# Memory columns and key weights in three parts, norm weights first on the queue, token scale spread later

## The chip, the core and the metric

The kernel runs on one core of a Trainium2 chip. The metric is the device time of one execution in microseconds (us). Three runs of the kernel before gave 1145.51, 1147.50 and 1147.76 us, a median of 1147.5.

The core's engines work in parallel, each through its own list of instructions: TensorE (PE, matmuls), VectorE (DVE), ScalarE (ACT), GpSimd (POOL) and SyncE (SP, which here issues nearly all transfers from memory). They meet through semaphores.

## What is computed

An encoder trunk of two layers over 256 tokens of width 1024, in fp32. Cut to what matters here:

```python
mem_n = rms_norm(mem, mem_norm)
for i in range(DEPTH):                       # 2 layers
    h = rms_norm(x, norm_mix[i])
    mkv = mem_n @ w_mem_kv[i]                # keys and values of the memory
    if i % 2 == 0:
        u = h @ na_w_in[j]                   # neighbourhood attention, layer 0
        ...
    else:
        mix, mq = gla_mixer(...)             # gated linear attention, layer 1
    att = memory_attention(mq, mkv)
    x = x + jnp.concatenate([mix, att], axis=-1) @ w_out[i]
    x = x + hierarchical_moe(rms_norm(x, norm_ffn[i]), ...)   # 32 experts, 2 per token
return rms_norm(x, final_norm)
```

The norm of a token is a factor for the token (the scale) times a weight for each feature. The kernel applies the two at different times: the weight to the transposed activations as soon as they are there, the scale of the memory tokens only to the keys and values that come out.

## The kernel before

The weights, about 440 MB, are read once. They pass through a ring in on-chip memory of eleven slots of 2 MB. SP issues the transfers in the order of use and waits before each for its slot; PE counts up `ring_used` as it finishes with weights.

The feature dimension of 1024 is cut into eight chunks of 128 (`KC`, index k). The memory tokens come as columns, `memT` (chunk by chunk, 256 tokens each), and are multiplied by key weights `mem_kw0` in `mem_k(0)` (L791 to L809). Columns and key weights arrive in two halves: chunks 0 to 3, then 4 to 7, in four transfers of 512 KB (L574 to L577). DVE multiplies chunks 0 to 3 by the norm weights, two at a time (L2096 to L2098), ACT chunks 4 to 7, one at a time (L1674 to L1677). PE waits for the DVE parts with `n_hT`, for all of ACT's with `n_hTa`, and for the key weights with `landed_kv0`. The norm weights of all norms, `gcol`, 28 KB, are the first transfer that ACT issues (L1460); a part of the constants (`cst`, with the identity and the matrix of ones) is its second.

PE's order at the start: four matmul calls on zeros (L1192 to L1195), `mem_k(0)`, `mem_v(0)` (L818 to L833: memory values, in two tiles of 128 tokens, eight chunks each), the memory queries (L1199 to L1205), the memory scale in every row (L1206, `scale_rows(1, 3)`), then the token values of attention (L838). Between the two tiles of `mem_v(0)` stands `scale_rows(0, TOKENB)` (L811 to L816). It waits for two diagonal matrices that DVE makes of the token scales (L1867), which rest on ACT's sums of squares over the token rows `xres` (L1496), and multiplies them by ones, so that every row holds the scale of all tokens. DVE needs this to scale and weight the eight chunks of token columns `hT0` (L2103 to L2108); the memory queries wait for chunks 0 to 3 and then for chunks 4 to 7 of them.

Behind the memory part SP issues, in this order: memory values' weights, token rows, token columns, query weights, memory rows, constants, value weights (L688 to L695), the weights of queries and keys (L698) and more. `piece_in` holds three semaphores for pieces of the last expert weights of each layer; PE waits for them at L1144 and L1146, long after the start.

fp32 matmul calls show as two instructions each in the trace.

Of the kernel before, what the change touches and what calls it, by code (L numbers as in the profile page):

```python
# [14 lines left out]
T = 256  # L15
# [42 lines left out]
TOKENB = 4  # L58
# [122 lines left out]
def build(nc, x, mem, final_norm, gla_out_norm, moe_w1, moe_w3, moe_w2, consts, mem_columns, x_columns, mem_keys, mem_values, mem_queries0,  # L181
          values0, queries_keys0, values1, values1_second, mem_queries1, queries_keys1, gates1, out0, out1, gains,
          logit_weights, logit_biases, gate_biases, gate_ups, biases0, first_up, last_up, last_down, out):
    with ExitStack() as ctx:
        def sb(name, shape, dt=F32):
            return ctx.enter_context(nc.sbuf_tensor(name, shape, dt))

        def sem(name):
            return ctx.enter_context(nc.semaphore(name))


        ring = sb("ring", [P, SLOTS * SLOT])
        cst = sb("cst", [P, C_END])
        gcol = sb("gcol", [P, 7, KC])
# [140 lines left out]
        s_x, s_mem, s_cst, s_rpb, s_small = sem("x_in"), sem("mem_in"), sem("const_in"), sem("rpb_in"), sem("small_in")  # L335
        s_gain = sem("gains_in")
# [12 lines left out]
        ring_in = [sem(f"ring_in{i}") for i in range(SLOTS + 1)]  # L349
# [58 lines left out]
        rt_p = sem("positions")  # L408
        rt_n = sem("rounds")
        again = [sem(f"positions_kept_and_last_group_selected_again{i}") for i in range(2)]  # L410
        piece_in = [sem(f"{name}_in") for name in ("third_slice_half0", "third_quarter", "third_slice_last_quarter")]

        class Quads:

# [31 lines left out]
        def quarter_columns(slot):  # L446
            return slot_view(slot).rearrange("p (q j e n) -> p q j e n", q=2, j=2, e=E4)
# [123 lines left out]
        @block.sync  # L571
        def _(sp):
            memT_rows = memT.rearrange("p k t -> p (k t)")
            for half in range(2):  # L574
                c, w = slice(half * 4 * T, (half + 1) * 4 * T), slice(half * 4 * 256, (half + 1) * 4 * 256)
                sp.dma_start(memT_rows[:, c], mem_columns[:, c]).then_inc(ring_in[(10, 9)[half]], 16)
                sp.dma_start(ring[:, w], mem_keys[0][:, w]).then_inc(ring_in[(8, 0)[half]], 16)  # L577

            def free(l, n):

# [189 lines left out]
        def _(pe):  # L770
            def arrived(a):
                pe.wait_ge(*a)
# [18 lines left out]
            def mem_k(l):  # L791

                w = mem_kw0 if l == 0 else kw1
                if l == 0:
                    arrived(landed_kv0[0])
                else:
                    arrived(landed_k1)
                    pe.wait_ge(s_memT, 1)
                for k0 in (0, 4):
                    if l == 0 and k0 == 4:  # L800
                        arrived(landed_kv0[1])
                        pe.wait_ge(n_hTa, TT)
                    for m in range(MPAIR):
                        for k in range(k0, k0 + 4):
                            if (l, m) == (0, 0) and k in (0, 2):
                                pe.wait_ge(n_hT, k // 2 + 1)
                            t = pe.matmul(ps[:, KB[l], m * T:(m + 1) * T], w[:, k, m * P:(m + 1) * P], memT[:, k, :],
                                          start=(m, k) == (0, 0), stop=(m, k) == (MPAIR - 1, KC - 1))
                t.then_inc(kv_mm, 1)  # L809

            def scale_rows(nth, bank):  # L811

                for a in range(TT):
                    pe.wait_ge(s_diag0, TT * nth + a + 1)
                    t = pe.matmul(ps[:, bank, a * P:(a + 1) * P], ones, diag0[:, a, :], start=True, stop=True)
                t.then_inc(s_rbc0, 1)  # L816

            def mem_v(l):  # L818

                w = mem_vw[l]  # L820
                if l == 0:
                    pe.wait_ge(s_memv, 16)
                else:
                    slot, there = main[0].fill(0, KV_AT * FILLS)
                    pe.wait_ge(ring_in[slot], there)
                for a in range(TT):
                    if l == 0 and a == 1:
                        pe.wait_ge(s_cst, 16)
                        scale_rows(0, TOKENB)
                    for k in range(KC):  # L830
                        t = pe.matmul(ps[:, VB[l], a * 256:a * 256 + 256], memT[:, k, a * P:(a + 1) * P], w[:, k, :],  # L831
                                      start=k == 0, stop=k == KC - 1)
                t.then_inc(ring_used, 1)  # L833
# [281 lines left out]
            def last_pieces(rn, l, c, slot, there):  # L1115

                w = quarter_columns(slot)
# [23 lines left out]
                pe.wait_ge(rn.sig.selwT_ready, c + 1)  # L1141
                pe.wait_ge(rn.sig.yb_ready, c * 2 + l + 1)
                scatter(rn, 0, 512, PIECES[0][3])
                pe.wait_ge(piece_in[1], 16 * (l + 1))  # L1144
                piece(1, 1).then_inc(rn.sig.down_half, 1)
                pe.wait_ge(piece_in[2], 16 * (l + 1))  # L1146
                piece(2, 0)
                if l == 0:
                    pe.wait_ge(rn.sig.added, c * 4 + 1)
# [307 lines left out]

        @block.scalar
        def _(act_e):
            act_e.dma_start(gcol[:], gains).then_inc(s_gain, 16)  # L1460
            act_e.dma_start(cst[:, 0:256], consts[:, 0:256]).then_inc(s_cst, 16)
            def table(func):

# [368 lines left out]
        def _(dve):  # L1832
# [261 lines left out]
            dve.wait_ge(s_gain, 16)  # L2094
            dve.wait_ge(ring_in[10], 16)
            for k in (0, 2):  # L2096
                V.tensor_tensor(memT[:, k:k + 2, :], memT[:, k:k + 2, :],
                                gcol[:, GAIN[0], k:k + 2].unsqueeze(2).to_broadcast([P, 2, T]), ALU.mult).then_inc(n_hT, 1)  # L2098
            dve.wait_ge(s_cst, 16)
# [95 lines left out]
            for i in range(2):  # L2195
                r, c = slice(i * CH, (i + 1) * CH), slice(i * CH, (i + 1) * CH)
# [72 lines left out]
```

## Time and profile before

| | |
|---|---|
| median of three runs | 1147.5 us (1145.51 to 1147.76) |
| span of the profiled execution | 1146.5 us |
| PE busy | 855.9 us (75%) |
| DVE busy, ACT busy | 208.9 us (18%), 179.1 us (16%) |
| moved by DMA | 444.48 MB, mean 388 GB/s |
| mean granted clock of TensorE | 0.881 |

The profile is of one execution. A busy share is a mean over stages with different limits, so it does not say what an edit in one stage is worth; for that the stage's own rows are read. A timeline row gives the start, the length, the engine, the line, what is written and read, and how many instructions were merged; in brackets stands how long the engine was idle ahead of it and what ended that. Matmuls overlap their successors, so that the distance between two starts tells more than the length of a row. A granted clock of 1.00 is 2.4 GHz, 0.50 is 1.2 GHz.

### The profile page before, as it was taken

The page shows a single profiled execution, that of the slowest core. Times are in us where ns is not written, and L with a number is a line of the kernel's source. Part 1 is how long each engine was busy: PE and PEld are TensorE (multiplying, and loading weights), DVE is VectorE, ACT ScalarE, POOL GpSimd, SP SyncE. Part 2 cuts the span into 40 slices and gives each one's busy share as a digit, 9 for nine tenths or more (in the row PEclk, how much of TensorE's full clock was granted, in tenths as well). Part 3 has the DMA queues.
Part 4 walks back from the last instruction along what each step waited for, and adds up shares of the span by engine and source line. Part 5 has one row for each costly group of instructions (what it writes and reads, how often), then busy time and mean ns, then how long its engine had stood idle before and what let it go on. Part 6 is the DMA issues. An engine that isn't in the chain of part 4 may idle for free.

```text
span 1146.5 us, 11577 instructions
## 1 busy us (share of the span) xinstructions
PE 855.9 (75%) x5102; PEld 401.9 (35%) x5102; DVE 208.9 (18%) x402; ACT 179.1 (16%) x384; POOL 19.2 (2%) x20
## 2 busy tenths in 40 slices
PE   9999997674948376757799999976565665664677
PEld 7687553221413121212258666322121221221222
DVE  2223231010101010101016634211010101010011
ACT  3333111010101000000036432100010100000002
POOL 0500000000000000000000000000000000000000
PEclk9999998896988778888999999988787888888887
DMA  9973799999999999999995658999999999999996
GB/s 375 420 297 112 281 380 412 429 429 428 426 427 428 428 425 428 430 429 427 421 424 216 258 222 334 421 428 428 428 428 427 429 427 426 428 428 427 428 426 245
DMA packets 36857, 444.48 MB, mean 388 GB/s; under 512 B 4545, under 2 KB 5057, under 8 KB 8002
## 3 DMA queue, kind: packets, MB, share of 16 engines
q1 hardware_dynamic: 36224, 443.16, 92.4%
q8 instruction: 43, 0.70, 0.2%
q10 hardware_dynamic: 578, 0.52, 0.1%
q14 instruction: 12, 0.10, 0.0%
HBM read 442.62 MB, written 1.05 MB: 387 GB/s over the span
## 4 chain that ended last, share of the span: by engine, by line
PE 53%; DMA 41%; ACT 2%; issue 2%; DVE 1%; SPq 0%; DVEq 0%
DMA ring<-in_moe_w 35%; PE ps L1026 12%; PE ps L1030 9%; PE ps L838 5%; PE ps L1235 4%; PE ps L917 3%; PE ps L998 3%; PE ps L1012 3%; DMA ring<-in_last_up 3%; DMA ring<-in_last_down 2%; PE ps L1325 2%; PE ps L924 2%; PE ps L1291 1%; DMA xres<-in_x 1%; PE ps L831 1%
## 5 line engine op out<-in xcount | busy, mean ns | idle before, releaser
L1026 PE MATMUL ps<-ring,work 128*32 128x512 f32 x2032 | 255.3, 658 | 138.3 <-DMA ring<-in_moe_w 117.1
L1030 PE MATMUL ps<-ring,work 128*32 128x512 f32 (+1 forms) x1024 | 141.8, 714 | 107.8 <-DMA ring<-in_moe_w 104.4
L1026 PEld LDWEIGHTS ps<-ring,work 128*32 128x32 f32 x2032 | 75.9, 119 | 303.3 <-issue 284.4
L1030 PEld LDWEIGHTS ps<-ring,work 128*32 128x32 f32 x1024 | 38.6, 131 | 200.0 <-issue 192.7
L2056 DVE TENSOR_TENSOR xres<-xres,ps 128x512 f32<-128x512 f32 (+1 forms) x64 | 42.9, 671 | 295.5 <-PE ps L998 292.9
L1012 PE MATMUL ps<-xs,work 128*128 128x512 f32 x112 | 54.5, 632 | 11.9 <-issue 9.5
L998 PE MATMUL ps<-work 128*128 128x512 f32 x120 | 55.7, 606 | 0.4 <-ACT work L1612 0.4
L838 PE MATMUL ps<-ring 128*128 128x384 f32 x160 | 53.3, 489 | 0.0
L2047 DVE TENSOR_TENSOR work<-work,ps 128x512 f32<-128x512 f32 x16 | 11.0, 688 | 231.9 <-PE ps L1026 231.9
L1625 ACT COPY work<-ps 128x512 f32<-128x512 f32 x28 | 16.4, 585 | 219.4 <-PE ps L1030 219.4
L1603 ACT COPY work<-ps 128x256 f32<-128x256 f32 x16 | 5.9, 372 | 247.6 <-PE ps L1063 247.6
L1235 PE MATMUL ps<-ring 128*128 128x256 f32 x192 | 43.0, 382 | 0.0
L917 PE MATMUL ps<-ring 128*128 128x512 f32 x88 | 39.1, 595 | 0.0
L1235 PEld LDWEIGHTS ps<-ring 128*128 128x128 f32 x192 | 36.0, 190 | 5.8 <-issue 0.9
L2018 DVE TENSOR_TENSOR work<-ps,gcol 128x512 f32<-128x512 f32 (+1 forms) x34 | 20.9, 655 | 92.3 <-PE ps L1017 90.0
L838 PEld LDWEIGHTS ps<-ring 128*128 128x128 f32 x160 | 29.8, 190 | 20.8 <-issue 1.4
L1012 PEld LDWEIGHTS ps<-xs,work 128*128 128x128 f32 x112 | 22.4, 203 | 42.0 <-issue 38.4
L998 PEld LDWEIGHTS ps<-work 128*128 128x128 f32 x120 | 21.5, 189 | 34.0 <-issue 34.0
L2044 DVE TENSOR_TENSOR work<-work,ps 128x512 f32<-128x512 f32 x16 | 11.0, 687 | 118.7 <-ACT work L1601 118.7
L1601 ACT ACTIVATE work<-ps 128x512 f32<-128x512 f32 x16 | 9.6, 597 | 138.0 <-PE ps L1026 138.0
L1599 ACT COPY work<-ps 128x512 f32<-128x512 f32 x28 | 16.4, 585 | 89.7 <-PE ps L1012 89.7
L917 PEld LDWEIGHTS ps<-ring 128*128 128x128 f32 x88 | 16.2, 190 | 18.0 <-issue 18.0
(273 smaller groups left out, 688.3 us busy)
## 6 DMA issues: line engine op xcount, KB each, us to landing
ring<-in_moe_w SPq DMA_DIRECT2D x161, 2048.0 KB, 30.8
ring<-in_last_up SPq DMA_DIRECT2D x8, 2048.0 KB, 34.3
ring<-in_moe_w SPq DMA_DIRECT2D x14, 1024.0 KB, 6.7
ring<-in_first_up SPq DMA_DIRECT2D x5, 2048.0 KB, 11.6
ring<-in_out SPq DMA_DIRECT2D x4, 2048.0 KB, 27.5
ring<-in_last_down SPq DMA_DIRECT2D x4, 2048.0 KB, 36.1
ring<-in_queries_keys SPq DMA_DIRECT2D x7, 1024.0 KB, 25.8
ring<-in_first_up SPq DMA_DIRECT2D x4, 1024.0 KB, 7.6
```

The source lines that it names most:

```text
L838: t = pe.matmul(ps[:, bank, 0:w.shape[-1]], hTs[l][:, k, a * P:(a + 1) * P], w[:, k, :], start=k == 0, stop=k == KC - 1)
L917: t = pe.matmul(ps[:, WOB[l][a] + half, :], mixTs[l][:, c, a * P:(a + 1) * P], out_rows(l, c, half), start=c == first, stop=c == last)
L924: t = pe.matmul(ps[:, WOB[l][1] + half, :], mixTs[l][:, c, P:2 * P], out_rows(l, c, half), start=False, stop=c == 5)
L998: pe.matmul(ps[:, banks[a], 0:n], selwT[:, a, :], yb[:, c0:c0 + n], start=True, stop=True).then_inc(rn.sig.scattered, 1)
L1012: t = pe.matmul(ps[:, half, :], sel[:, a].rearrange("p e s -> p (e s)"), xs[:, a, half * 512:half * 512 + 512], start=a == 0, stop=a == TT ...
L1026: return pe.matmul(ps[32 * e:32 * e + 32, 4 + m, :], xsel[:, k, 32 * e:32 * e + 32], w, start=k == 0, stop=k == KC - 1, tile_position=(0, ...
L1030: return pe.matmul(ps[32 * e:32 * e + 32, bank, 0:w.shape[-1]], actT[:, j, 32 * e:32 * e + 32], w, start=j == 0, stop=j == 3, tile_positio ...
L1235: t = pe.matmul(ps[:, p % 2, t_ * T:(t_ + 1) * T], qkw[p][t_][:, k, :], hT0[:, k, :], start=k == 0, stop=k == KC - 1)
L1325: t = pe.matmul(ps[:, 4 + j, t_ * T:(t_ + 1) * T], qkw1[t_][j][:, k, :], hT1[:, k, :], start=k == 0, stop=k == KC - 1)
L1599: nc.scalar.copy(xrow[:, half * 512:half * 512 + 512], ps[:, half, :]).then_inc(rn.sig.picked_sb, 1)
L2018: V.tensor_tensor(xsel[:, k0:k0 + n, :], ps[:, bank, 0:n * P].rearrange("p (k t) -> p k t", t=P), gcol[:, 2 + 2 * l, k0:k0 + n].unsqueeze( ...
L2056: V.tensor_tensor(cols, cols, ps[:, banks[a], 0:n], ALU.add).then_inc(rn.sig.added, 1)
```

## The change

The norm weights move from ACT's first issue to SP's first issue, ahead of the memory columns. The memory columns and key weights come in three parts, chunks 0-1, 2-3 and 4-7, six transfers instead of four. The second parts report on two of the `piece_in` semaphores, which are renamed and whose later waits count 16 higher. DVE waits for the second columns before its second operation, PE for the second keys before chunk 2. `mem_k` runs in three parts for both layers. `scale_rows(0, TOKENB)` moves from ahead of tile 1 of the memory values to behind the first four chunks of that tile.

```diff
@@ sync @@
-            for half in range(2):
-                c, w = slice(half * 4 * T, (half + 1) * 4 * T), slice(half * 4 * 256, (half + 1) * 4 * 256)
-                sp.dma_start(memT_rows[:, c], mem_columns[:, c]).then_inc(ring_in[(10, 9)[half]], 16)
-                sp.dma_start(ring[:, w], mem_keys[0][:, w]).then_inc(ring_in[(8, 0)[half]], 16)
+            sp.dma_start(gcol[:], gains).then_inc(s_gain, 16)
+            for (k0, k1), mem_there, keys_there in (((0, 2), ring_in[10], ring_in[8]), ((2, 4), s_mem2, s_keys2),
+                                                    ((4, 8), ring_in[9], ring_in[0])):
+                c, w = slice(k0 * T, k1 * T), slice(k0 * 256, k1 * 256)
+                sp.dma_start(memT_rows[:, c], mem_columns[:, c]).then_inc(mem_there, 16)
+                sp.dma_start(ring[:, w], mem_keys[0][:, w]).then_inc(keys_there, 16)
@@ tensor, mem_k @@
-                for k0 in (0, 4):
+                for k0, k1 in ((0, 2), (2, 4), (4, 8)):
+                    if l == 0 and k0 == 2:
+                        pe.wait_ge(s_keys2, 16)
                     if l == 0 and k0 == 4:
                         arrived(landed_kv0[1])
                         pe.wait_ge(n_hTa, TT)
                     for m in range(MPAIR):
-                        for k in range(k0, k0 + 4):
+                        for k in range(k0, k1):
@@ tensor, mem_v @@
                 for a in range(TT):
-                    if l == 0 and a == 1:
-                        pe.wait_ge(s_cst, 16)
-                        scale_rows(0, TOKENB)
                     for k in range(KC):
+                        if l == 0 and (a, k) == (1, 4):
+                            pe.wait_ge(s_cst, 16)
+                            scale_rows(0, TOKENB)
@@ tensor, last pieces @@
-                pe.wait_ge(piece_in[1], 16 * (l + 1))
+                pe.wait_ge(piece_in[1], 16 * (l + 2))
...
-                pe.wait_ge(piece_in[2], 16 * (l + 1))
+                pe.wait_ge(piece_in[2], 16 * (l + 2))
@@ scalar @@
-            act_e.dma_start(gcol[:], gains).then_inc(s_gain, 16)
@@ vector @@
             for k in (0, 2):
+                if k == 2:
+                    dve.wait_ge(s_mem2, 16)
                 V.tensor_tensor(memT[:, k:k + 2, :], memT[:, k:k + 2, :],
```

## Rows read from the trace of the kernel before

**Rows 1.** The page, part 4: chain that ended last, shares by engine.

```profile
PE 53%; DMA 41%; ACT 2%; issue 2%; DVE 1%; SPq 0%; DVEq 0%
```

**Rows 2.** Stretches: span, length, each engine's busy us, clock, DMA share, GB/s.

```profile
core 0: us, PE busy (x) PEld busy (x) DVE busy (x) ACT busy (x) POOL busy (x), PEclk, DMA share, GB/s
0.00:55.00 55.00, 52.75 (x215) 37.12 (x216) 13.84 (x30) 18.32 (x43) 17.20 (x17) 1.00 0.98 397
...
113.00:154.00 41.00, 40.44 (x179) 23.15 (x174) 14.55 (x45) 11.62 (x24) 0.00 (x0) 1.00 0.79 309
...
215.00:570.00 355.00, 226.77 (x1397) 81.49 (x1397) 37.52 (x62) 25.43 (x46) 0.00 (x0) 0.83 1.01 427
...
585.00:695.00 110.00, 109.85 (x551) 74.85 (x550) 49.06 (x61) 45.22 (x91) 1.97 (x3) 1.00 0.69 274
```

**Rows 3.** Waits of SP's queue, 50 to 250 us: us, times, longest.

```profile
SPq L666 <- PE ps L860: 13.4, 1, 13.4
```

**Rows 4.** Timeline of PE, first 8 us: start, us, what [idle before].

```profile
5.08 1.33 PE L1195 MATMUL ps<-work 128*128 128x256 f32 x4
6.85 1.35 PE L807 MATMUL ps<-work,ring 128*128 128x256 f32 x5 [0.44 <-DMA ring<-in_mem_keys]
```

**Rows 5.** Timeline of PE, 13 to 30 us.

```profile
13.86 3.62 PE L831 MATMUL ps<-ring,work 128*128 128x256 f32 x16
17.32 0.38 PE L815 MATMUL ps<-work,cst 128*128 128x128 f32 x2
17.96 0.49 PE L815 MATMUL ps<-work,cst 128*128 128x128 f32 x2 [0.26 <-DVE work L1867]
18.29 3.62 PE L831 MATMUL ps<-ring,work 128*128 128x256 f32 x16
21.74 7.07 PE L1203 MATMUL ps<-ring 128*128 128x256 f32 x32
28.65 0.61 PE L815 MATMUL ps<-work,cst 128*128 128x128 f32 x4
29.09 1.13 PE L838 MATMUL ps<-ring 128*128 128x384 f32 x3
```

**Rows 6.** Timeline, 0 to 60 us: scaling by DVE and ACT, the last diagonal.

```profile
5.40 1.29 DVE L2097 TENSOR_TENSOR work<-work,gcol 128x512 f32<-128x512 f32 x2 [3.94 <-DMA gcol<-in_gains]
...
8.30 1.70 ACT L1675 ACTIVATE work<-work,gcol 128x256 f32<-128x256 f32 x4 [5.13 <-DMA work<-in_mem_columns]
...
17.62 0.29 DVE L1867 TENSOR_SCALAR work<-cst,st 128x128 f32<-128x128 f32 x1
...
18.56 3.22 DVE L2105 SCALAR_TENSOR_TENSOR ring<-ring,gcol,ps 128x256 f32<-128x256 f32 x8 [0.65 <-PE ps L815]
```

**Rows 7.** Timeline of SP's issues: first columns, second columns, second keys.

```profile
0.75 0.38 SPq L576 DMA_DIRECT2D work<-in_mem_columns  x1
...
1.66 0.42 SPq L576 DMA_DIRECT2D work<-in_mem_columns  x1
2.13 0.58 SPq L577 DMA_DIRECT2D ring<-in_mem_keys  x1
```

**Rows 8.** Line 576, memory columns: from issue to landing.

```profile
DMA to landing us min/median/max: 4.4/5.5/6.5
```

**Rows 9.** Line 577, key weights: from issue to landing.

```profile
DMA to landing us min/median/max: 5.6/6.5/7.3
```

**Rows 10.** Stretch of half a microsecond, columns as in rows 2.

```profile
2.00:2.50 0.50, 0.50 (x1) 0.00 (x1) 0.00 (x0) 0.50 (x1) 0.00 (x0) 1.00 0.75 198
```

**Rows 11.** Line 695, value weights, issued from 6.15 us: from issue to landing.

```profile
DMA to landing us min/median/max: 21.6/22.8/24.0
```

**Rows 12.** Line 735, first store of the output: from issue to landing.

```profile
DMA to landing us min/median/max: 2.0/2.0/2.0
```

**Rows 13.** Timeline of PE: up projection at 161 us and in the tail.

```profile
161.68 7.08 PE L1026 MATMUL ps<-ring,work 128*32 128x512 f32 x64
...
1115.87 3.64 PE L1026 MATMUL ps<-ring,work 128*32 128x512 f32 x16 [1.81 <-DMA ring<-in_last_up]
```

More of the change, by code:

```diff
@@ L410, in build @@
         again = [sem(f"positions_kept_and_last_group_selected_again{i}") for i in range(2)]
-        piece_in = [sem(f"{name}_in") for name in ("third_slice_half0", "third_quarter", "third_slice_last_quarter")]
+        piece_in = [sem(f"{name}_in") for name in ("third_slice_half0", "memory_columns_2_3_then_third_quarter",
+                                                   "memory_keys_2_3_then_third_slice_last_quarter")]
+        s_mem2, s_keys2 = piece_in[1], piece_in[2]
         class Quads:
```

## Prediction

> **What bounds the kernel now.** I read the chain of work that ended last first: PE 53%, DMA 41% [rows 1]. The split by stage says which holds where [rows 2]: in 0 to 55 us PE is busy for 52.75 us at a granted clock of 1.00 (the 2.4 GHz level), and so it is in 113 to 154 and 585 to 695; in 215 to 570 the DMA share is 1.01 at 427 GB/s and PE is busy for 227 of 355 us: there the expert weights set the pace. The change touches only the first 30 us, a stage set by PE. Does a microsecond won there reach the end, with a stage behind it that is bound by DMA? In 113 to 154 the DMA share is only 0.79, since SP waits for ring slots that PE frees; the longest such wait for the next stream of weights is 13.4 us, for the last transposes of attention [rows 3]. So the long stream starts when PE lets it, and what PE gains early moves the stream, and then all behind it, by the same amount.
>
> Next the first 30 us of PE, in order of time [rows 4, 5]. Warm-up matmuls run to 6.41. The first memory matmul starts at 6.85, after 0.44 us of idle that ended with the landing of the key weights. Then 32 instructions (16 matmul calls, two each) run without a gap, at (13.86 - 6.85) / 32 = 0.22 us each. The memory values take 16 instructions (tile 0), 13.86 to 17.32; then come the four instructions that spread the token scale. The second pair of them waits for DVE; tile 1 starts at 18.29, which is 0.97 us after 17.32. The same four instructions without a wait take 29.09 - 28.65 = 0.44 us. So this wait costs PE 0.53 us. The memory queries (L1203) start at 21.74. The whole visible idle that the change can take is therefore 0.44 + 0.53 = 0.97 us.
>
> **Part 1: smaller transfers and norm weights first.** Before, DVE scaled memory chunks 0 to 3 at 5.40 to 6.69, released by the norm weights, not by the columns (issued at 0.75, landed 4.4 us later, 5.15) [rows 6 to 8]. With only chunks 0 and 1 in front (256 KB and 256 KB instead of 512 and 512) the first keys no longer wait for the second half of their own transfer. The two landings in the queue before were 512 KB apart and 1.2 to 1.6 us apart: columns 5.15, keys 6.8, columns 1.66 + 6.5 = 8.16, keys 2.13 + 7.3 = 9.43 [rows 4, 7 to 9]. Half of that spacing is 0.6 to 0.8 us for 256 KB, so the first keys should land near 5.2 to 5.6, under the warm-up's end at 6.41, the DVE operation of 0.65 us before it too. PE then starts at 6.41, or, since matmul records overlap their successors, as early as 6.25 (last warm-up matmul at 6.03 plus 0.22). Chunks 2 and 3 are needed 8 instructions later, at 8.0 to 8.2; they land where the first MB landed before, near 6.8, and are scaled before that. Nothing stalls.
>
> What is late next is the third part. ACT scales chunks 4 to 7 in four operations, 8.30 to 10.00, and starts when the columns land (8.16) [rows 6, 8]. PE reached them at 6.85 + 16 x 0.22 = 10.4 before, so ACT was covered by 0.4 us. Now PE would be there at 9.8 to 10.0 and waits for ACT until 10.05. Hence the gain at this point is 10.43 - 10.05 = 0.38 us, not 0.44 to 0.6, less every delay d of the third columns. The third keys (9.43 + d) are in time for d below 0.6.
>
> How large is d? The bytes ahead of the third columns are the same; what is new is three more issues on SP, 0.44 us each [rows 7]: the third columns are issued about 1.3 us later (norm weights, then five transfers). Lower bound 0: they already took 6.5 us from issue to landing, nearly all of it behind other bytes. Upper bound 1.3: the issue time decides in full. In between: the queue is short of work only in its first microseconds, when it moved 198 GB/s against 397 on average over 0 to 55 [rows 2, 10]. The one issue put ahead of the first columns costs at about half rate 0.44 x 0.5 = 0.2 us. The third columns' row is nearer to the lower bound, since the queue is never empty again, so d = 0.2. All later transfers (token rows, token columns, values) shift by the same d.
>
> A rule of the Trainium skill speaks against this part. The trace shows a smallest time from issue to landing of 2.0 us, for an output store on an idle queue [rows 12], yet landings in a filled queue 1.2 to 1.6 us apart. "DMA: Bandwidth & Descriptors", section "Rules for kernel authors", asks for at least 1 MiB per DMA, and the section on the anatomy of one DMA gives a fixed 2.0 us for each. If each paid that alone, an estimate from that page would be 3 x 2.0 = 6 us of delay; the landing rows do not bear it out, as four transfers would then be over 2 us apart.
>
> **Part 2: token scale spread later.** It moves behind the first four chunks of tile 1, 8 instructions or 1.73 us later on PE. The values of tile 0 start at 13.86 - 0.38 + d = 13.48 + d, tile 1 at 16.94 + d, the scale at 18.67 + d. The diagonals are ready at 17.91 + d [rows 6], so the wait of 0.53 us is gone, with 0.76 us to spare. But DVE's scaling of the token columns (L2105, eight operations in 3.22 us) starts later: before it came 0.11 us after the end of the second pair (17.96 + 0.49 = 18.45); all four in a row last 0.61. That is 18.67 + 0.61 + 0.11 = 19.39 + d, against 18.56. Four of eight are done at 19.39 + 1.61 = 21.00 + d, and 0.06 for the signal (my estimate from DVE's end at 17.91 and PE's start at 17.96) makes 21.06 + d. PE itself is done with tile 1 at 18.67 + 0.44 + 1.73 = 20.84 + d. So a small new wait of 0.22 us stands ahead of L1203, on DVE. The second four are done at 22.67 + d, and PE wants them at 21.06 + 1.73 = 22.79 + d: just in time. L1203 starts at 21.06 + d instead of 21.74: the sum is -0.68 + d, with d = 0.2 **-0.48 us**.
>
> Behind it: L838 needs the second half of the values, which landed at 6.15 + 21.6 = 27.8 [rows 11]; PE asks now at 28.6 (29.09 before). With d = 0.2 it lands at 28.0: covered by 0.6 us. The two new waits of PE (chunks 2 and 3) and the split loop, also run once for layer 1 with the same 32 instructions, cost 0 to 0.1 us; I take 0. ACT's second issue starts 0.44 us earlier and its constants are wanted only for the diagonals, of which the last is made at 17.62: nothing. The other counts of the reused semaphores cost nothing: the same waits at the same places.
>
> The profiled execution has a span of 1146.5 us; the median of the runs is 1147.5, so about 1.0 lies around the span. 1146.5 - 0.48 = 1146.0, plus 1.0 gives 1147.0 us.
>
> **Rivals.**
> (a) The issues decide (d from 0.4 to 1.3). At d = 0.68 the gain is gone: the third columns land at 8.84 or later and PE stands before them. At d = 1.3 the kernel is slower by 0.62: 1148.1. For it: six issues of 0.44 us one after another. Against it: 6.5 us from issue to landing. Chance 0.16.
> (b) Slower by more than can be overlooked: every transfer pays its own start. With 2.0 us from the store's row for each of the three additional ones, d = 6.0, and L1203 comes 5.3 us later: 1152.8. It decides from d = 0.68 and passes 0.2% of the time from d = 3.0. This is also the time by the skill's rule. The spacing of landings speaks against it: 0.03.
> (c) The gain does not reach the end: somewhere between 120 and 215 us the stream is kept by its own bytes. Then 1147.5. The 13.4 us wait of SP speaks against it: 0.09.
> (d) TensorE's clock in the tail. The last L1026 group runs 16 instructions in 3.64 us, at a granted clock of 0.50 (1.2 GHz), right after PE's waits for the last weights; the same form took 7.08 us for 64 at 1.00, so 1.77 for 16 [rows 13]. A shift of all events by 0.5 us may move the fall or rise of the clock. If it does not fall, this group gains 1.87 us and the next ones some 1.3: 1143.7. Chance 0.06. If it rises only after 1133 instead of 1125, up to 7 us of full-rate work runs slower, half of it taken: 1150.5. Chance 0.05.
>
> **How the numbers follow.** The forecast, -0.68 to -0.28, has the remaining 0.61. A measurement of this kernel can tell about 0.2% (2.3 us) from no change; its own runs span 2.25 us. Forecast, (a) and (c) lie within that; (d) has 0.06 below and 0.05 above, (b) 0.03 above; the runs' scatter adds 0.05 to faster and leaves 0.01 for slower. So faster 0.11, same 0.80, slower 0.09. The range takes the scatter about the forecast and (a): 1144.4 to 1149.0.
>
> **What would show it.** PE's first memory matmul at 6.25 to 6.45, no idle to DMA; a short idle ahead of its 17th instruction, ended by ACT L1675 or its columns; the four scale instructions without idle between them, from about 18.9; DVE's L2105 at 19.6; L1203 at 21.26 with about 0.2 us of idle; the wait of SP for the last transposes ending about 0.5 us earlier than 124.3. A third landing of columns after 9.0 would show (a); landings 2 us apart (b). A time beyond the range would have to come with another pattern of clock, or with a DMA rate other than 427 GB/s in the long stretches; then my claim that only the shift matters is wrong.

## Result: slower by 0.2%, from transfers that land late in the first microseconds

In 15 runs each, the changed kernel took 1148.98 us in the median (1145.8 to 1152.07) and the kernel before 1147.32 us (1144.49 to 1148.96). The ratio is 1.0019, with a 95% interval of 1.0010 to 1.0027: slower by 1.1 to 3.1 us. I had forecast 1147.0 and a small gain. The time lies just inside my range, but the movement goes the other way and is clear of the noise.

PE's timeline in the changed kernel shows where it begins (start, length, instructions, idle before; it answers to [rows 4, 5]):

```profile
5.90 1.89 PE L813 MATMUL ps<-work,ring 128*128 128x256 f32 x8
8.64 2.00 PE L813 MATMUL ps<-work,ring 128*128 128x256 f32 x8 [0.85 <-DMA ring<-in_mem_keys]
12.07 3.69 PE L813 MATMUL ps<-work,ring 128*128 128x256 f32 x16 [1.44 <-ACT work L1680]
15.60 5.34 PE L837 MATMUL ps<-ring,work 128*128 128x256 f32 x24
20.78 0.61 PE L821 MATMUL ps<-work,cst 128*128 128x128 f32 x4
21.22 1.89 PE L837 MATMUL ps<-ring,work 128*128 128x256 f32 x8
23.30 7.15 PE L1209 MATMUL ps<-ring 128*128 128x256 f32 x32 [0.18 <-DVE ring L2112]
```

PE starts the memory keys at 5.90 instead of 6.85, a gain of 0.95 us. Eight instructions later it waits for the second keys, and eight later again for ACT. The third part starts at 12.07, 1.7 us after the time (about 10.4) at which the kernel before had reached the same chunks. The token scale runs without a wait, as intended, and L1209, the memory queries, starts at 23.30 instead of 21.74. The loss is in the landings of the transfers. ACT and the token rows, with SP's issues (answering to [rows 6, 7]):

```profile
0.75 0.38 SPq L576 DMA_DIRECT2D gcol<-in_gains  x1
1.19 0.42 SPq L580 DMA_DIRECT2D work<-in_mem_columns  x1
1.66 0.42 SPq L581 DMA_DIRECT2D ring<-in_mem_keys  x1
...
3.08 0.43 SPq L580 DMA_DIRECT2D work<-in_mem_columns  x1
...
10.22 1.70 ACT L1680 ACTIVATE work<-work,gcol 128x256 f32<-128x256 f32 x4 [7.53 <-DMA work<-in_mem_columns]
16.43 1.06 ACT L1501 ACTIVATE xs<-xres 128x1024 f32<-128x1024 f32 x1 [4.50 <-DMA xres<-in_x]
```

ACT's scaling of the last columns starts at 10.22 (8.30 before), the first work on the token rows, when they land, at 16.43 (14.54 before). So the last memory columns and the token rows behind them land 1.9 us later, and so do the memory rows (ACT's work on them starts at 23.98 instead of 22.09). The stretches of two microseconds show when the queue fell behind (columns as in [rows 2]). Before:

```profile
4.00:6.00 2.00, 2.00 (x5) 1.14 (x4) 0.60 (x1) 0.00 (x0) 0.00 (x0) 1.00 1.00 381
6.00:8.00 2.00, 1.56 (x7) 1.06 (x7) 0.69 (x2) 0.00 (x0) 0.00 (x0) 1.00 1.02 384
8.00:10.00 2.00, 2.00 (x11) 1.74 (x11) 0.00 (x0) 1.70 (x4) 0.00 (x0) 1.00 1.05 438
```

And after:

```profile
4.00:6.00 2.00, 2.00 (x7) 1.20 (x6) 0.69 (x1) 0.00 (x0) 0.00 (x0) 1.00 0.89 271
6.00:8.00 2.00, 1.78 (x9) 1.23 (x7) 0.69 (x1) 0.00 (x0) 0.00 (x0) 1.00 0.79 215
8.00:10.00 2.00, 1.36 (x6) 1.23 (x7) 0.00 (x0) 0.00 (x0) 0.00 (x0) 1.00 1.04 409
```

Between 2 and 4 us the changed kernel was ahead (287 GB/s against 205). Between 4 and 8 us its queue moved 215 to 271 GB/s instead of 381 to 384, and the DMA engines were busy only 0.79 to 0.89 of the time, though SP had issued more than 2 MB by then. Idle engines are only part of it: 215 GB/s at a share of 0.79 would be 272 at a full share, against 376 before (384 / 1.02), so the engines also moved fewer bytes while they were busy. From 8 us on the rates are nearly the same again.

The bytes account for about half of the 1.9 us. Over the first 20 us the queue moved 331 GB/s on average, against 352 before, which is 0.42 MB less, or 1.0 us at the 410 to 430 GB/s of the stretches behind; over the first 30 us (361 against 375) it is still 0.42 MB. The other half is order. When the token rows landed, 5.13 MB had been moved in the changed kernel (312 GB/s over 16.43 us) and 4.77 MB before (328 over 14.54), although the bytes needed until then are the same: more of the later transfers was already done. No run shows why.

From there the delay goes with PE. SP's wait for the last transposes is the same 13.4 us as in [rows 3], only later (it ends at 125.92 instead of 124.29), the first expert matmul starts at 155.74 instead of 154.12, the long stretches run at the same rate (427 GB/s), and the tail's L1032 group starts 1.94 us later than in [rows 13]. The two profiled executions nevertheless have the same span, 1146.5 us. The tail says why. After:

```profile
1117.81 3.55 PE L1032 MATMUL ps<-ring,work 128*32 128x512 f32 x16 [2.97 <-DMA ring<-in_last_up]
...
1123.67 1.93 PE L1036 MATMUL ps<-ring,work 128*32 128x512 f32 x24 [0.68 <-ACT work L1610]
```

Before, the second of these groups was

```profile
1122.20 3.42 PE L1030 MATMUL ps<-ring,work 128*32 128x512 f32 x24 [0.68 <-ACT work L1605]
```

The same 24 instructions took 1.93 us in one execution and 3.42 in the other: the granted clock was back at 1.00 (2.4 GHz) from 1122 on after, and only from about 1125 on before. The two small groups ahead of it gained as well. What decides this is open: the second trace of the changed kernel has 1.93 us too, and of the 14 other kernels below eight have the short group and six a long one of 3.0 to 3.6 us, with the same matmuls in the tail of all. The medians do not share the gain.

### The profile page after: what moved, and what is told of

Same layout as the page of the kernel before. It is cut to its first block, busy times and chain, and to the rows that moved or that the text cites. A ratio compares the mean times of both kernels' runs of the same rounds, so it can differ in the third digit from the quotient of the medians.

```text
span 1146.5 us, 11580 instructions
## 1 busy us (share of the span) xinstructions
PE 861.0 (75%) x5102; PEld 403.1 (35%) x5102; DVE 209.1 (18%) x402; ACT 179.1 (16%) x384; POOL 19.2 (2%) x20
## 4 chain that ended last, share of the span: by engine, by line
PE 49%; DMA 47%; ACT 1%; DVE 1%; issue 1%; SPq 0%; DVEq 0%; ACTq 0%
DMA ring<-in_moe_w 41%; PE ps L1032 13%; PE ps L1036 8%; PE ps L844 5%; PE ps L1241 4%; PE ps L923 3%; DMA ring<-in_last_up 3%; DMA ring<-in_last_down 2%; PE ps L1331 2%; PE ps L1004 2%; PE ps L930 2%; PE ps L1018 1%; PE ps L1297 1%; PE ps L813 1%; PE ps L949 1%
## 5 line engine op out<-in xcount | busy, mean ns | idle before, releaser
L1032 PE MATMUL ps<-ring,work 128*32 128x512 f32 x2032 | 262.1, 673 | 131.6 <-DMA ring<-in_moe_w 111.1
L1036 PE MATMUL ps<-ring,work 128*32 128x512 f32 (+1 forms) x1024 | 138.3, 699 | 107.7 <-DMA ring<-in_moe_w 104.6
L1032 PEld LDWEIGHTS ps<-ring,work 128*32 128x32 f32 x2032 | 77.3, 122 | 302.1 <-issue 283.9
L1018 PE MATMUL ps<-xs,work 128*128 128x512 f32 x112 | 57.6, 663 | 11.5 <-issue 9.2
```

Of the source, the lines that this page charges most:

```text
L1018: t = pe.matmul(ps[:, half, :], sel[:, a].rearrange("p e s -> p (e s)"), xs[:, a, half * 512:half * 512 + 512], start=a == 0, stop=a == TT ...
L1032: return pe.matmul(ps[32 * e:32 * e + 32, 4 + m, :], xsel[:, k, 32 * e:32 * e + 32], w, start=k == 0, stop=k == KC - 1, tile_position=(0, ...
L1036: return pe.matmul(ps[32 * e:32 * e + 32, bank, 0:w.shape[-1]], actT[:, j, 32 * e:32 * e + 32], w, start=j == 0, stop=j == 3, tile_positio ...
```

## Experiments

Two markers of a trace do not depend on the tail: the time at which the token rows land (ACT's first work on them) and the start of the first expert matmul. In three kernels with the same transfers as before (the kernel before, `e3_scale_later`, `e6_pe_delay`) the token rows landed at 14.54, 14.67 and 14.83, so 0.3 us is the scatter of the first marker. A difference from the one trace of the kernel before can be too large by as much. The bytes moved in the first 20 us scatter less: these three kernels have a mean of 351 to 352 GB/s, so they are the third marker, "queue".

The texts on record name theories by letters. P: packets of 2 KB are slow. N: each additional issue of SP delays all behind it. G: norm weights ahead of the columns hold the queue up. W: each transfer over all engines costs the queue 0.5 to 0.8 us at the start. T: the moment at which the first megabyte stands in the queue decides. S: transfers of 256 KB are slower at the start. C: the two queues disturb each other. The diffs show only the lines that matter, with "..." where lines are left out.

All numbers of the experiments (us; "queue" in GB/s):

| kernel | token rows | last columns scaled from | memory queries | first expert matmul | queue | ratio (95%) |
|---|---|---|---|---|---|---|
| before | 14.54 | 8.30 | 21.74 | 154.12 | 352 | |
| after | 16.43 | 10.22 | 23.30 | 155.74 | 331 | 1.0019 (1.0010 to 1.0027) |
| f3_after_again | 16.24 | 10.03 | 23.10 | 155.74 | 327 | 1.0016 (1.0002 to 1.0030) |
| e1_gains_first | 15.38 | 9.15 | 22.57 | 154.94 | 344 | 1.0014 (1.0001 to 1.0027) |
| e2_three_parts | 15.70 | 9.46 | 22.90 | 155.55 | 333 | 1.0011 (1.0000 to 1.0022) |
| e3_scale_later | 14.67 | 8.46 | 21.54 | 153.99 | 351 | 1.0001 (0.9988 to 1.0014) |
| e4_rows_split | 17.08 | 10.86 | 25.58 | 158.08 | 307 | 1.0028 (1.0014 to 1.0042) |
| e5_keys_on_act | 16.36 | 11.36 | 25.20 | 157.77 | 343 | 1.0024 (1.0013 to 1.0036) |
| e6_pe_delay | 14.83 | 8.60 | 24.94 | 157.76 | 352 | 1.0026 (1.0016 to 1.0037) |
| e7_small_packets | 14.14 | 7.92 | 21.34 | 153.72 | 357 | 1.0002 (0.9991 to 1.0014) |
| e8_tiny_issues | 14.53 | 8.32 | 21.73 | 154.63 | 352 | 1.0009 (0.9996 to 1.0022) |
| f1_five_tiny | 15.08 | 8.85 | 22.28 | 154.65 | 349 | 1.0004 (0.9992 to 1.0015) |
| f2_small_wide | 15.04 | 8.80 | 22.23 | 154.98 | 346 | 1.0004 (0.9994 to 1.0014) |
| e9_best | 14.29 | 8.06 | 21.66 | 154.12 | 350 | 1.0005 (0.9997 to 1.0014) |
| g1_slow_first_mb | 15.24 | 9.02 | 22.44 | 155.07 | 339 | 1.0007 (0.9995 to 1.0018) |
| g2_after_cst_late | 16.97 | 10.72 | 23.80 | 156.24 | 317 | 1.0012 (0.9998 to 1.0026) |
| g3_second_half_split | 15.37 | 8.38 | 22.57 | 155.25 | 346 | 1.0008 (0.9996 to 1.0020) |

In `g3_second_half_split` 8.38 is for chunks 4 and 5; chunks 6 and 7 are scaled from 9.65.

### The parts of the change one by one

`e1_gains_first`: only the norm weights' place.

```diff
+            sp.dma_start(gcol[:], gains).then_inc(s_gain, 16)      # SP, first
-            act_e.dma_start(gcol[:], gains).then_inc(s_gain, 16)   # ACT, first
```

> The kernel before with one part of the change alone: the norm weights are SP's first issue instead of ACT's; still two halves of columns and keys, scale spread early. The disputed number is the start of ACT's scaling of the last columns, which follows their landing: 8.30 us before, 10.22 after, with L1203 (memory queries) at 21.74 and 23.30. Theory P (the packets of 2 KB of the small transfers are slow): no such packets here, ACT starts at 8.3 to 8.5 and memory queries at 21.2 to 21.7. Theory N (each additional issue of SP delays all that stands behind it): one issue more, 0.44 us, so ACT at 8.6 to 8.8. Theory G (norm weights ahead of the columns hold the queue up): ACT at 9.5 to 10.2. Total within 0.1% of before by P and N, up to 2 us slower by G.

Measured: token rows at 15.38, last columns scaled from 9.15. This is between N and G: 0.84 us for one issue of 0.44 us, or 0.55 against the latest of the three traces with unchanged transfers (14.83).

`e2_three_parts`: only the six transfers instead of four, with the waits that go with them.

```diff
-            for half in range(2):
+            for (k0, k1), mem_there, keys_there in (((0, 2), ...), ((2, 4), ...), ((4, 8), ...)):
```

> The kernel before with the three parts of columns and keys alone: six transfers, norm weights still issued by ACT, scale spread early. P and N: nearly the whole loss is here, ACT's scaling starts at 9.6 to 10.2, memory queries at about 23 to 23.7 (no gain from a later scale, but the wait for the diagonals is hidden as PE is late itself); the total is 1.2 to 2.5 us slower. G: ACT at 8.3 to 8.7, memory queries at 21.7 to 22.

Measured: token rows 15.70 (1.16 us later), scaling from 9.46, memory queries 22.90. The two parts add up within the scatter: 0.84 + 1.16 = 2.0 against 1.89 for the whole change. So "nearly the whole loss is here" was wrong; the norm weights carry about two fifths of it. The stretch from 6 to 8 us shows that idle engines are not needed for the loss:

```profile
6.00:8.00 2.00, 2.00 (x10) 1.73 (x9) 0.69 (x1) 0.00 (x0) 0.00 (x0) 1.00 0.94 224
```

The engines were busy for 0.94 of it and moved 224 GB/s, where the kernel before moved 384 at 1.02.

`e3_scale_later`: only the later spread of the token scale.

```diff
-                    if l == 0 and a == 1:
...
+                        if l == 0 and (a, k) == (1, 4):
```

> The kernel before with the token scale spread behind four chunks of tile 1, and nothing else. All theories of the loss lie in the transfers, so this alone should gain: scale instructions without a wait at 19.05, memory queries at 19.05 + 0.61 + 0.11 + 1.61 + 0.06 = 21.44 instead of 21.74, and at 154 us the experts' first matmuls 0.3 us earlier. In the total 0.3 us cannot be told from nothing (ratio 0.999 to 1.001).

```profile
19.02 0.61 PE L815 MATMUL ps<-work,cst 128*128 128x128 f32 x4
19.46 1.89 PE L831 MATMUL ps<-ring,work 128*128 128x256 f32 x8
21.54 7.14 PE L1203 MATMUL ps<-ring 128*128 128x256 f32 x32 [0.18 <-DVE ring L2105]
```

PE's timeline of this kernel: no wait at the scale, a new one of 0.18 us on DVE ahead of L1203, and L1203 0.20 us earlier than before, experts 0.13. The mechanism of part 2 holds, its worth is 0.1 to 0.2 us, and the total shows nothing.

### Does PE's start reach the end?

`e6_pe_delay`: PE delayed alone, the transfers as before.

```diff
-            for _ in range(2):
+            for _ in range(12):
                 pe.matmul(ps[:, 7, 0:256], zeros[:, 0:P], zeros[:, 0:256], start=True, stop=True)
```

> The kernel before with ten more warm-up matmul calls of 256 columns on zeros (20 instructions at 0.22 us, 4.4 us), which only delay PE: the transfers stay as they are. PE's first memory matmul moves from 6.85 to about 10.65, memory queries from 21.74 to about 25.0, the first expert matmuls from 154.1 to 157.4. If PE's start sets the start of the long weight stream, as the prediction says, the total is 3.3 us slower (ratio 1.0028); the rival is that the stream goes by its own bytes, and then the total stays (ratio 0.999 to 1.001).

Memory queries at 24.94 (3.20 us later), experts 3.64 us later, total 1.0026 (1.8 to 4.2 us). PE's delay passes through. The rival "the gain does not reach the end", (c) of the prediction, falls.

### What makes the landings late?

`e7_small_packets`: packets of 2 KB, but no additional transfer.

```diff
+                        sp.dma_start(dst[:, 0:1024].rearrange("p (b n) -> p b n", b=2), blocks[:, 0:4:3]).then_inc(there, 16)
```

> The kernel before with four transfers of 512 KB in the same order, but the two first halves are read from memory in two pieces of 2 KB per row (blocks of two chunks stored in another order, results unchanged), so their packets are 2 KB, as in the change; no additional issue. Theory P: ACT's scaling of the last columns starts at 9.0 to 9.6 instead of 8.30, memory queries at 22.5 to 23. Theory N: 8.3 to 8.5 and 21.6 to 21.9.

Token rows at 14.14, scaling from 7.92, the earliest of all kernels. The packets of the first halves were of 2 KB here too and nothing was lost, so the theory of the small packets falls.

`e4_rows_split`: the same count and sizes of transfers as in the change, but packets of 4 KB, since the first halves are cut by partitions.

```diff
+            for half, rows, mem_there, keys_there in ((0, slice(0, 64), ...), (0, slice(64, 128), ...), (1, slice(0, 128), ...)):
```

> The kernel before with its first halves of columns and keys each cut by partitions (64 and 64) instead of by chunks: six transfers of the same sizes as in the change, issued in the same places, but each row keeps its 4 KB; both parts are awaited together, norm weights on ACT, scale early. It tells the packets' size from the number of transfers. P: the last columns land as before, ACT's scaling at 8.3 to 8.7, memory queries at 21.7 to 22.0. N: as with the three parts, ACT at 9.6 to 10.2 and memory queries at 23 or later.

Token rows at 17.08, later still than with the three parts. It speaks against P, but it does not count cleanly for N, because a transfer over 64 partitions is slow by itself:

```profile
4.00:6.00 2.00, 2.00 (x5) 1.08 (x4) 0.00 (x0) 0.00 (x0) 0.00 (x0) 1.00 1.07 204
6.00:8.00 2.00, 0.85 (x3) 0.27 (x1) 0.00 (x0) 0.00 (x0) 0.00 (x0) 1.00 1.04 221
```

Here the engines are fully busy (1.04 to 1.07) and move about half the bytes; in the changed kernel they are idle in part as well.

`e5_keys_on_act`: the changed kernel with the key weights issued by ACT.

```diff
-                sp.dma_start(ring[:, w], mem_keys[0][:, w]).then_inc(keys_there, 16)
+                act_e.dma_start(ring[:, k0 * 256:k1 * 256], mem_keys[0][:, k0 * 256:k1 * 256]).then_inc(keys_there, 16)
```

> The changed kernel with the three key transfers issued by ACT instead of SP (norm weights and columns stay on SP): the same six transfers with the same packets, but two engines issue at once, so the last columns are issued at about 2.1 us instead of 3.08, and all that SP issues behind them 1.4 us earlier. ACT's scaling of the last columns started at 10.22 in the changed kernel. Theory N (the issues of SP set the pace): it starts at 8.8 to 9.3, memory queries at 22 instead of 23.3. Theory P (packets of 2 KB, or the number of transfers in the queue whoever issues them): 9.8 to 10.3, memory queries at 23 or later.

All theories missed. The token rows land as in the changed kernel (16.36 against 16.43) although SP issued them 1.1 us earlier (3.50 against 4.58), and the columns come later. By then ACT had issued all keys (the third ones at about 1.7), so that they may have shared the engines with the columns; that is my reading and was not tried by itself:

```profile
9.62 0.69 DVE L2105 TENSOR_TENSOR work<-work,gcol 128x512 f32<-128x512 f32 x1 [3.39 <-DMA work<-in_mem_columns]
11.36 1.70 ACT L1681 ACTIVATE work<-work,gcol 128x256 f32<-128x256 f32 x4 [7.21 <-DMA work<-in_mem_columns]
```

The memory queries, at 25.20, carry more than this: PE waited 2.12 us for the second columns, and from 12 to 14 us the granted clock was 0.50.

`e8_tiny_issues` and `f1_five_tiny`: two or five transfers of 4 bytes between the halves.

```diff
+                if half == 0:
+                    for i in range(2):      # 5 in f1
+                        sp.dma_start(tiny[0:1, i:i + 1], consts[0:1, i:i + 1]).then_inc(s_out, 16)
```

> The kernel before with two transfers of 4 bytes each issued by SP between the first and the second half, which nobody waits for during the work: two more issues of about 0.44 us, no more bytes, packets of 4 KB. Theory N: ACT's scaling of the last columns starts 0.9 to 1.2 us later, at 9.2 to 9.5, memory queries at 22.6 to 23. Theory P: 8.3 to 8.5 and 21.7.

> The kernel before with five transfers of 4 bytes between the halves, on one partition each, so each uses one DMA engine: the last columns are issued at about 3.2 us, even later than in the changed kernel (3.08), and nothing is added to the other fifteen engines. Theory N (issue time decides, with a threshold that the two tiny ones did not pass): ACT's scaling of the last columns starts at 9.5 to 10.3 and the token rows land 1.5 us later. Theory W (each whole transfer, spread over all 16 engines, costs the queue 0.5 to 0.8 us in its first microseconds; single-engine ones cost nothing): ACT at 8.3 to 8.7, memory queries at 21.7 to 22.1.

With two, the last columns were issued at 2.30 and nothing landed later (14.53), which refutes N for two issues. With five:

```profile
1.67 1.64 SPq L581 DMA_DIRECT2D tiny<-in_consts  x5
3.35 0.36 SPq L577 DMA_DIRECT2D work<-in_mem_columns  x1
```

The last columns are issued at 3.35, later than in the changed kernel, and yet they are scaled from 8.85 and the token rows land at 15.08: 1.69 us of delay in the issue cost 0.54 (0.25 against the latest trace with unchanged transfers), and the mean over 20 us fell only from 352 to 349 GB/s. N and W both missed (9.5 or more, 8.7 or less). A late issue behind a full first megabyte is mostly hidden. This also refutes my rival (a) in its simple form.

`f2_small_wide`: two transfers of 18 KB over all partitions in the same place.

```diff
+                if half == 0:
+                    sp.dma_start(rbias[:, 0], logit_biases[:, 0]).then_inc(s_small, 16)
+                    sp.dma_start(rbias[:, 1], logit_biases[:, 1]).then_inc(s_small, 16)
```

> The kernel before with its logit biases, 36 KB, moved between the halves and cut in two, so that two small transfers over all 128 partitions and 16 engines stand there: 18 KB each, 36 KB more ahead of the last columns (0.1 us at 400 GB/s), last columns issued 0.9 us later. Theory W: ACT's scaling of the last columns starts at 9.3 to 10.0, like that of the three parts alone (9.46). If only bytes and the size of the data transfers count: 8.4 to 8.6. Theory N: 8.3 to 8.5 too, since two tiny issues did not delay it.

Token rows at 15.04 and scaling from 8.80, as with five tiny ones and later than the 8.4 to 8.6 for bytes alone. The two cost 0.50 us together, so a fixed price of 0.5 to 0.8 us for each whole transfer, as theory W had it (scaling from 9.3 or later), is not there.

`f3_after_again`: the changed kernel, a second trace.

> The changed kernel once more, for a second trace of its first microseconds. If the late landing belongs to the kernel, ACT's scaling of the last columns starts at 9.9 to 10.5 again and memory queries at 23.0 to 23.6, and the total is 1.5 to 3 us slower than before; if it was a chance of one execution, ACT starts at 8.3 to 9.5.

It repeats: 16.24, 10.03, 23.10, ratio 1.0016. The late landing belongs to the kernel.

`g1_slow_first_mb`: four transfers of 512 KB, but issued at the pace of the three parts.

```diff
+                for i in range(2) if half == 0 else ():      # between first columns and first keys
+                    sp.dma_start(tiny[0:1, i:i + 1], consts[0:1, i:i + 1]).then_inc(s_out, 16)
                 sp.dma_start(ring[:, w], mem_keys[0][:, w]).then_inc(ring_in[(8, 0)[half]], 16)
+                if half == 0:
+                    sp.dma_start(tiny[0:1, 2:3], consts[0:1, 2:3]).then_inc(s_out, 16)
```

> The kernel before with two transfers of 4 bytes (one engine each) between the first columns and the first keys, and one behind the keys: the four data transfers stay 512 KB, but the first megabyte is all issued only at 2.1 us and the last columns at about 2.6, the schedule that the three parts have. Token rows landed at 14.54 us before and 15.70 with the three parts. Theory T (the moment at which the first megabyte stands in the queue decides, about 1 us for each): token rows at 15.3 to 15.9, ACT's scaling of the last columns at 9.2 to 9.7. Theory S (transfers of 256 KB are themselves slower at the start than ones of 512 KB): 14.7 to 15.1 and 8.4 to 8.9, as with five tiny ones behind the first megabyte (15.08).

```profile
4.00:6.00 2.00, 2.00 (x5) 1.13 (x4) 0.86 (x2) 0.00 (x0) 0.00 (x0) 1.00 1.03 365
6.00:8.00 2.00, 1.66 (x9) 1.13 (x8) 0.43 (x1) 0.00 (x0) 0.00 (x0) 1.00 0.81 227
```

Token rows at 15.24. Its first keys were issued at 1.83 instead of 1.19, its last columns at 2.55, so earlier than in `f1_five_tiny` (3.35). The loss at the token rows, 0.70 us against 0.54 there, does not separate the two, since 0.16 us is less than the scatter. The bytes do: 339 GB/s over 20 us against 349, which is 0.6 us of work lost against 0.15, and there is the same hole between 6 and 8 us as in the changed kernel (227 GB/s at a share of 0.81), which `f1_five_tiny` does not have:

```profile
4.00:6.00 2.00, 2.00 (x5) 1.08 (x4) 0.37 (x1) 0.00 (x0) 0.00 (x0) 1.00 1.01 385
6.00:8.00 2.00, 1.80 (x7) 1.14 (x6) 0.92 (x2) 0.00 (x0) 0.00 (x0) 1.00 1.02 363
```

The value lies just under the span of T (15.3 to 15.9) and above that of S. If the two kernels may be compared so, the schedule of the first megabyte makes 0.7 of the 1.16 us of the three parts, and the rest remains with the smaller transfers.

`g3_second_half_split`: the second halves cut instead of the first.

```diff
+            for (k0, k1), mem_there, keys_there in (((0, 4), ...), ((4, 6), ...), ((6, 8), ...)):
```

> The kernel before with its second halves cut instead of its first: chunks 0-3 in one piece, then 4-5 and 6-7, six transfers, the first megabyte issued by 1.6 us as before. T: only the small price of later issues behind the first megabyte, token rows at 14.7 to 15.1. S: 1.2 us later as with the three parts, token rows at 15.5 to 16.0. PE waits for both pieces together.

Token rows at 15.37, between T and S again. The first megabyte was issued as early as before, with its keys at 1.19, and still 0.83 us was lost; so the schedule of the first megabyte is not the whole cause.

`g2_after_cst_late`: the changed kernel without ACT's 128 KB in the first microseconds.

```diff
-            act_e.dma_start(cst[:, 0:256], consts[:, 0:256]).then_inc(s_cst, 16)
+            sp.dma_start(cst[:, 0:256], consts[:, 0:256]).then_inc(s_cst, 16)   # behind the token rows
```

> The changed kernel with the 128 KB of constants taken from ACT's queue to SP's, behind the token rows: no other queue competes in the first microseconds. Token rows landed at 16.43 in the changed kernel (16.24 in its second trace). Fewer bytes ahead are worth 0.3 us: T and S both expect 15.9 to 16.2, last columns scaled from 9.7 to 9.9. Theory C (the two queues disturb each other): 15.0 to 15.5 and 8.6 to 9.2.

All three theories missed: with less ahead of them the last columns were scaled from 10.72, 0.5 us later than in the changed kernel, and the mean over 20 us fell to 317 GB/s. So ACT's transfer is not what holds SP's queue up. Why it went slower without it is not known; it is one trace.

`e9_best`: a try for a faster version.

```diff
-            act_e.dma_start(cst[:, 0:256], consts[:, 0:256]).then_inc(s_cst, 16)
+            sp.dma_start(cst[:, 0:256], consts[:, 0:256]).then_inc(s_cst, 16)   # behind the token rows
...
+                        if l == 0 and (a, k) == (1, 4):
```

> A try for a faster version: the kernel before with the later spread of the token scale, and with the constants that ACT issued (128 KB, wanted only at 16 us) on SP's queue behind the token rows. 128 KB less ahead of the memory columns is 0.3 us at 400 GB/s: first keys at 6.5 instead of 6.8, last columns at 7.9 instead of 8.2, memory queries at 21.1 to 21.3 instead of 21.74. The total gains 0.3 to 0.6 us, which cannot be told from nothing (0.999 to 1.001). If a whole transfer that moves onto SP's queue costs 0.5 us or more there (theory W), token rows and diagonals come later, and memory queries at 21.5 or later.

Experts at 154.12, exactly as before, ratio 1.0005. Last columns at 8.06 and token rows at 14.29 are each 0.24 us earlier, which is within the scatter, and PE's start stayed at 6.78. The memory queries came at 21.66, not at the 21.1 to 21.3 that I expected; that is on W's side of the line, but not for W's reason, since the token rows did not come later. No version found here beats the kernel before by more than the noise.

## Why the prediction was wrong

**Read right.** The start is bound by PE, and a shift of PE there reaches the end: `e6_pe_delay` shows it, and over all kernels the ratio rises, on the whole, with the first expert matmul's time. The step from DMA's waits for freed slots [rows 3] to "the stream starts when PE lets it" held. Part 2 held in its mechanism, with the new wait on DVE measured at 0.18 us against 0.22 worked out, and a gain of 0.20 us at L1203 against 0.3. The first memory matmul came earlier than I said (5.90; 6.17 in the second trace), and the third part became the gate, as I had it.

**The step that failed.** The term d, the delay of the third columns and all behind them, for which I took 0.2 us and an upper bound of 1.3, measured 1.9 (1.7 in the second trace). With it, my own formula gives -0.68 + 1.9 = +1.2 us at L1209, where +1.56 was measured. The difference of 0.34 us is 0.12 at the third part (placed at 10.05 + d = 11.95, measured 12.07), 0.08 up to DVE's L2112 (19.39 + d = 21.29, measured 21.49) and 0.14 from there to L1209. So the mechanism was that of rival (a), to which I gave 0.16, with a size beyond its end. I bounded it by the issue times alone: the transfers cannot be later than the issues that stand ahead of them. But the third columns were issued 1.42 us later (3.08 against 1.66) and landed 1.9 us later. The parts show two errors in this. First, the norm weights ahead of the columns cost 0.84 us (at least 0.55) for an issue of 0.44, which I took at half. Second, an issue is not a fixed price: 1.69 us of delay behind the first megabyte cost the queue 0.15 us of bytes in 20 us, whereas 0.64 us inside it, with 0.89 for the last columns, cost 0.6, and cutting the second halves, with the first megabyte on time, made the token rows 0.83 us later. Both the schedule of the first megabyte and the number or size of the transfers seem to count. I read "6.5 us from issue to landing, nearly all of it behind other bytes" [rows 8] as a full queue, and "the queue is never empty again" was not in the rows: the queue moved 198 GB/s then [rows 10], and later, in the changed kernel, 215 GB/s at a busy share of 0.79 between 6 and 8 us.

**The rule weighed against the trace.** The Trainium skill's advice of at least 1 MiB per DMA ("DMA: Bandwidth & Descriptors", "Rules for kernel authors") pointed the right way here. The price of 2.0 us for each transfer, my estimate of 6 us from that page (and rival (b), from the store's row), did not. That page of the Trainium skill gives its 2.0 us for transfers that GpSimd issues, which the prediction left out; these are issued by SP. The three additional transfers on SP's queue cost 1.9 us together, and `f2_small_wide` shows 0.5 for two small ones.

**Rival (d)**, the clock in the tail, occurred in part: the group that I had named still ran slowly (3.55 us against 3.64), but the next large one took 1.93 against 3.42. It hid the loss in the profiled execution and is a reason not to compare two spans.

**Open.** Why the queue moves so little between 4 and 8 us, with more than 2 MB issued, is not settled: the engines stand idle for a tenth to a fifth of the time and move fewer bytes while they are busy. Nor is it known why bytes of later transfers were moved ahead of the token rows' last ones. Excluded as the cause of the whole are the packets' size (`e7_small_packets`), the competing queue (`g2_after_cst_late`), a fixed cost of 0.5 us or more for each transfer (`f2_small_wide`) and the issue time of the last columns alone (`f1_five_tiny`). A slow issue of the first megabyte reproduces the hole (`g1_slow_first_mb`) and some 0.7 us of the loss, in one trace. How the rest is divided between smaller transfers and the schedule was not separated.

## What to carry to other kernels

At the start of a kernel, let no small transfer stand ahead of the first needed ones on their queue: 28 KB there cost 0.84 us here. Cutting the head of the queue brought the first piece earlier and the rest later; with the norm weights moved as well, PE began 0.95 us earlier and the rest landed 1.9 us later. Cut a first transfer only where the next gate, not the first one, has slack for it; here the gate of the third part had 0.4 us. Judge edits of a microsecond in a kernel of a millisecond by markers inside the trace, such as a landing and the first matmul of a stage, since spans also differ by the clock of the tail.

## What the runs showed of the hardware that I had not expected

Transfers over 64 of 128 partitions ran at little more than half the rate with the engines fully busy: 204 and 221 GB/s at shares of 1.07 and 1.04 in `e4_rows_split`, against 381 and 384 before. In the same kernel TensorE waited 2.71 us ahead of its first memory matmul and then ran at the lower clock level, as this stretch shows:

```profile
10.00:12.00 2.00, 2.00 (x7) 1.53 (x6) 0.00 (x0) 1.14 (x3) 0.00 (x0) 0.50 1.04 424
```

This is part of why its memory queries came 3.84 us later and the token rows only 2.54. In the changed kernel the two waits of 0.85 and 1.44 us did not lower it.

A DVE multiplication of 128x1024 on the attention scores took 1.23 us before and 1.93 us in `e8_tiny_issues`, where a POOL operation began just ahead of it rather than just behind it (39.10, against 39.27 before; DVE began at 39.16 and 39.17):

```profile
39.10 4.52 POOL L758 TENSOR_TENSOR ring<-ring 128x320 f32<-128x320 f32 x4 [4.80 <-DMA ring<-in_biases]
39.16 1.93 DVE L1906 TENSOR_TENSOR work<-work,st 128x1024 f32<-128x1024 f32 x1
```

It shifted the first expert matmul by 0.5 us although all was on time until 29.08. The other traces bear the order out. In the five kernels where DVE began first, the operation took 1.23 us. In the twelve where POOL's group began first it took 1.25 to 1.93, and in the nine of these where POOL was 0.06 to 0.74 us ahead, DVE ended 1.98 to 2.00 us after POOL's start: it took 1.67 us with 0.33 ahead in `e2_three_parts`, 1.25 with 0.74 in the changed kernel. An estimate from these is that DVE got nothing done in the first 0.76 us of POOL's operation (1.99 - 1.23). No run changed the order alone. So the first expert matmul's time can carry up to 0.5 us that does not come from the landings themselves.
